# Four-layer hybrid decoder on one core: where the sums of squares stand among the memory products, and who adds the squares

## The reference

```
def rms_norm(x, g):
    xf = x.astype(F32)
    y = xf * lax.rsqrt(jnp.mean(xf * xf, axis=-1, keepdims=True) + EPS)
    return (y * g.astype(F32)).astype(x.dtype)

def memory_kv(mem, g, w_k, w_v):
    m = rms_norm(mem, g)
    shp = mem.shape[:2] + (X_HEADS, X_HEAD_DIM)
    return (m @ w_k).reshape(shp), (m @ w_v).reshape(shp)
...
        x = x + rms_norm(y, g[1])
        h = rms_norm(x, g[2])
        y = memory_cross_attn(h, mem_k[layer], mem_v[layer], P['x_w_q'][layer], P['x_w_o'][layer])
        x = x + rms_norm(y, g[3])
```

## Time and profile before

| | us |
|---|---|
| median of 3 runs | 2017.05 |
| lowest and highest run | 2014.43, 2022.57 |
| span of the profiled execution | 2015.7 |
| TensorE busy | 1951.5 (97%) |
| VectorE busy | 1244.4 (62%) |
| ScalarE busy | 930.6 (46%) |
| GpSimd busy | 1008.8 (50%) |

### The profile page before, as it was taken

How to read it: one execution, slowest core, us unless ns; L and a number is a source line. 1 busy time by engine, 2 the same in 40 slices (tenths; PEclk the granted TensorE clock), 3 DMA queues, 4 the chain that set the end, 5 groups by cost and what they waited for, 6 DMA issues and landing times.

```text
span 2015.7 us, 35615 instructions
## 1 busy us (share of the span) xinstructions
PE 1951.5 (97%) x13890; PEld 1763.9 (88%) x13890; DVE 1244.4 (62%) x2220; ACT 930.6 (46%) x1557; POOL 1008.8 (50%) x1249
## 2 busy tenths in 40 slices
PE   7999999999999999999999999999999999999997
PEld 5998989798888988897889999999998889989976
DVE  5988342426887787755147777777454157874552
ACT  3676522334555555342354444443243347674333
POOL 4776704026555655250356666566631337776602
PEclk8999999999999999999999999999999999999998
DMA  4444476535444544487353444444586344445870
GB/s 130 149 147 135 135 250 231 208 105 174 124 116 132 151 132 140 138 297 241 113 170 108 130 130 130 137 136 146 165 313 211 132 148 141 135 148 166 292 231 27
DMA packets 332615, 324.64 MB, mean 161 GB/s; under 512 B 19768, under 2 KB 313056, under 8 KB 332448
## 3 DMA queue, kind: packets, MB, share of 16 engines
q1 hardware_dynamic: 330944, 321.49, 49.8%
q10 hardware_dynamic: 1504, 0.87, 0.2%
HBM read 292.16 MB, written 29.61 MB: 160 GB/s over the span
## 4 chain that ended last, share of the span: by engine, by line
PE 75%; DVE 14%; ACT 5%; issue 2%; DMA 2%; POOL 1%; SPq 1%; DVEq 0%; ACTq 0%
PE ps L773 10%; PE ps L774 10%; PE ps L778 10%; PE ps L1458 5%; PE ps L1467 4%; PE ps L1261 3%; PE ps L1524 2%; PE ps L888 2%; PE ps L763 2%; PE ps L765 2%; PE ps L764 2%; ACT wh L1713 2%; DVE work L2543 2%; PE ps L1602 1%; PE ps L1541 1%
## 5 line engine op out<-in xcount | busy, mean ns | idle before, releaser
L1693 POOL TENSOR_TENSOR wl<-raw,wh 128x256 fp32r<-128x256 f32 x1216 | 1003.3, 860 | 979.1 <-ACT wh L1713 978.9
L1713 ACT ACTIVATE wh<-raw 128x1024 fp32r<-128x1024 f32 x304 | 311.8, 1053 | 202.1 <-PE ps L778 49.8
L773 PE MATMUL ps<-Hh,wh 128*128 128x320 f32 x1200 | 372.2, 324 | 2.8 <-DVE work L2563 0.9
L774 PE MATMUL ps<-Hl,wh 128*128 128x320 f32 x1200 | 360.4, 314 | 0.0
L773 PEld LDWEIGHTS ps<-Hh,wh 128*128 128x128 f32 x1200 | 230.0, 192 | 11.3 <-DVE work L2427 2.3
L774 PEld LDWEIGHTS ps<-Hl,wh 128*128 128x128 f32 x1200 | 230.4, 192 | 2.1
L2258 DVE TENSOR_SCALAR work<-ps 128x512 f32<-128x512 f32 (+8 forms) x220 | 100.3, 474 | 170.9 <-PE ps L871 39.8
L778 PE MATMUL ps<-Hh,wl 128*128 128x320 f32 x1200 | 201.1, 310 | 0.0
L778 PEld LDWEIGHTS ps<-Hh,wl 128*128 128x128 f32 x1200 | 183.2, 189 | 0.1
L773 PE MATMUL ps<-Oh,wh 128*128 128x320 f32 x512 | 152.2, 310 | 3.7 <-DVE Ol L3004 3.7
L774 PE MATMUL ps<-Ol,wh 128*128 128x320 f32 x512 | 151.1, 308 | 0.0
(11 more groups left out here) (439 smaller groups left out, 3922.0 us busy)
## 6 DMA issues: line engine op xcount, KB each, us to landing
raw<-rg_w_in SPq DMA_DIRECT2D x128, 256.0 KB, 3.5
raw<-hg_w_in SPq DMA_DIRECT2D x128, 256.0 KB, 4.8
raw<-ssd_w_in SPq DMA_DIRECT2D x96, 256.0 KB, 3.9
work<-cache_mem_k SPq DMA_DIRECT2D x40, 512.0 KB, 6.3
work<-cache_mem_v SPq DMA_DIRECT2D x40, 512.0 KB, 5.1
raw<-rg_w_out SPq DMA_DIRECT2D x64, 256.0 KB, 3.6
raw<-x_w_k SPq DMA_DIRECT2D x64, 256.0 KB, 3.6
raw<-x_w_v SPq DMA_DIRECT2D x64, 256.0 KB, 3.7
```

The source lines that it names most:

```text
L773: pe.matmul(ps[:, bank, 0:n], high(half, k), mh[:, k, 0:n], start=(k == 0), stop=False)
L774: pe.matmul(ps[:, bank, 0:n], high(half, k), ml[:, k, 0:n], start=False, stop=False)
L1693: ins = pool.tensor_tensor(out, src, wh[:, parted(n) % HALVES, r:r + 2].bitcast(F32), ALU.subtract)
L1713: act.activation(wh[:, nx.n % HALVES], raw[:, slot, :, half * P:(half + 1) * P], ACT.Copy).then_inc(hi_ready, 1)
```

## The change

Three edits, all in the attention stages.

1. At a seam, `sum_squares(5 + 4 * L, 7)` becomes `sum_added`: VectorE adds the eight tiles of X's squares (seven additions behind its `residual`), and TensorE runs one product with ones in place of eight. The numbers of `sq_added` are counted anew (4 for each layer in place of 3). The sum moves from before the wait for `at_v_ready` to two steps of k behind it.
2. At a seam, `values(4, 0)` is cut in two: four steps of k stand before the first sum, four after it. The later `values(4, 0)` is cut at two steps around the second sum.
3. In attention 1 the first sum moves from behind `memory(0)` into the middle of `memory(1)`.

The sums write banks 6 and 7, the value products 4 and 5, the memory products 0 to 3, so a group of accumulations can stand open around a sum. ScalarE's, GpSimd's and SyncE's programs stay as they are.

```
--- before.py
+++ after.py
@@ -1441,7 +1441,7 @@
 
 
             def attention(L):
-                def memory(n):
+                def memory(n, ks=range(KD)):
                     block = units.n // 2
                     pe.wait_ge(landed[block % SLOTS], 64 * (block // SLOTS + 1))
                     if L != 1 and n < 4:
@@ -1452,21 +1452,22 @@
                         pe.wait_ge(*past("rg_so_ready", 8 * (1 if L == 0 else 2)))
                     if n >= 4:
                         pe.wait_ge(*past("at_kvt_ready", KD * L + n - 3))
-                    for k in range(KD):
+                    for k in ks:
                         if n == 0:
                             pe.wait_ge(*past("mem_normal", 2 * KD * L + k + 1))
                         mm = pe.matmul(ps[:, n % 4, 0:NMEM], raw[:, block % SLOTS, k, n % 2 * P:(n % 2 + 1) * P], memh[:, k, :],
                                        start=(k == 0), stop=(k == KD - 1))
-                    done(mm)
-
-                def values(bank, a):
+                    if KD - 1 in ks:
+                        done(mm)
+
+                def values(bank, a, ks=range(KD)):
 
                     block = units.n // 2
                     pe.wait_ge(landed[block % SLOTS], 64 * (block // SLOTS + 1))
-                    for k in range(KD):
+                    for k in ks:
                         mm = pe.matmul(ps[:, bank, 256 * a:256 * a + 256], memh[:, k, a * P:(a + 1) * P], raw[:, block % SLOTS, k, :],
                                        start=(k == 0), stop=(k == KD - 1))
-                    if a:
+                    if a and KD - 1 in ks:
                         done(mm, 2)
 
                 def turn_memory(h):
@@ -1480,11 +1481,16 @@
                             mm = pe.transpose(ps[:, 4 + h % 2, 256 * a + P * c:256 * a + P * (c + 1)], at_kt[:, t, a * P:(a + 1) * P], ident[:])
                     mm.then_inc(S("at_turned_full"), 1)
                 for n in range(KD):
-                    memory(n)
-                    if n == 0:
-                        sum_added(2 + 4 * L, 6, 3 * L + 1)
+                    if L == 1 and n == 1:
+                        memory(1, range(4))
+                        sum_added(2 + 4 * L, 6, 4 * L + 1)
+                        memory(1, range(4, KD))
+                    else:
+                        memory(n)
+                    if L != 1 and n == 0:
+                        sum_added(2 + 4 * L, 6, 4 * L + 1)
                     if n == 4:
-                        sum_added(3 + 4 * L, 7, 3 * L + 2)
+                        sum_added(3 + 4 * L, 7, 4 * L + 2)
                     if n % 2 == 1 and n >= 3:
                         turn_memory((n - 3) // 2)
                 if L == 0:
@@ -1612,16 +1618,18 @@
                         pe.wait_ge(*past("at_y_ready", KD * L + t - 3))
                     project(t % 4, t % 2, Oh, Ol)
                 if L == DEPTH - 1:
-                    sum_added(4 + 4 * L, 6, 3 * L + 3, (KD - 1,))
+                    sum_added(4 + 4 * L, 6, 4 * L + 3, (KD - 1,))
                     return
-                values(4, 0)
-                sum_added(4 + 4 * L, 6, 3 * L + 3, (KD - 1,))
+                values(4, 0, range(4))
+                sum_added(4 + 4 * L, 6, 4 * L + 3, (KD - 1,))
+                values(4, 0, range(4, KD))
                 values(4, 1)
                 values(5, 0)
                 values(5, 1)
-                sum_squares(5 + 4 * L, 7)
                 pe.wait_ge(*past("at_v_ready", XH * (L + 1) + 2))
-                values(4, 0)
+                values(4, 0, range(2))
+                sum_added(5 + 4 * L, 7, 4 * L + 4)
+                values(4, 0, range(2, KD))
                 values(4, 1)
 
             rg(0)
@@ -3004,6 +3012,8 @@
                     tt(sample_o(Ol), ps[:, 6 + hb, 0:256].rearrange("p (c h q) -> p c h q", c=2, h=XH), sample_o(Oh).bitcast(F32), SUB).then_inc(S("at_o_ready"), 1)
                 add_squares(4 + 4 * L, KD - 1)
                 residual(4 + 4 * L, gain(L, 3))
+                if L < DEPTH - 1:
+                    add_squares(5 + 4 * L)
 
                 wait("at_k_out0", (L + 1) * 32)
                 wait("at_k_out1", (L + 1) * 32)
```

## The result

| | before | after |
|---|---|---|
| median of 5 runs, us | 2017.05 | 1999.74 |
| lowest and highest, us | 2014.43, 2022.57 | 1996.85, 2007.11 |
| span of the profiled execution, us | 2015.7 | 1999.1 |
| TensorE busy, us | 1951.5 | 1935.4 |
| VectorE busy, us | 1244.4 | 1254.4 |

The ratio is 0.9925, 95% interval 0.9906 to 0.9943: 0.75% faster, 11.5 to 19 us. The forecast was faster by 10.49 us (0.52%). Its chances were nearly even, 0.47 for a gain beyond 0.5% and 0.51 for one within; the whole interval lies beyond.

A forecast was written before the change was run, and what follows sets the result against it. Seams were taken as bounded by the second sum's end plus 7.60 us, with TensorE busy 97%. Three seams at 2.91 us plus 1.76 us in attention 1 made 10.49 us: 2006.6 us forecast, range 2001.5 to 2013.5.

The forecast's parts named there:

- The bound of a seam: At each seam, the mixer starts 7.60 us after the second sum ends; 2.91 of 3.77 us removed arrive.
- The first half step: At a seam, the first sum moves 1.72 us earlier, to 430.78, its input ready 0.16 us before; no TensorE cost.
- The adds: At a seam, VectorE's seven additions run from 440.04 to 444.10 us, 0.7 us before TensorE sums, at no cost.
- C: At the seams, adds come late on slower VectorE, 6.6 us; a seam gives 1.0 us, total 2012.2 us; chance 0.06.
- Attention 1: At its start, the moved first sum fills TensorE's wait for VectorE's adds; gain 1.76 us, second sum fitting by 0.2.
- Idle time: Before the mixer, TensorE's wait grows to about 1.4 us at the first seam; weight-part waits total 4.4 us.
- B: The clock falls once at each of the three seams; 5.4 us gained, 2011.7 us; chance 0.08.
- D: The clock falls at a seam and stays low 10.4 us; 4.8 us slower, 2021.8 us; chance 0.04.
- the clock term: Clock loss at the seams' longer gaps, taken as none; the range keeps 1.7 us a seam.
- I find nothing with a fixed date: Behind the seams, waits and weight loads hang on the chain and move by the same 2.91 us, so the gain survives.
- 3 us to each side: Whole kernel: spread taken around the forecast case, for run spread and short clock falls.
- E: Behind the seams, their gain is handed back by a load or early sum; only 1.76 us stays, 2015.3; chance 0.06.

The follow-up runs named there:

- The early weight parts: Changed kernel with ScalarE making the high parts of the mixer's first two weight units before the second sum's root: ratio 0.9934, a seam of 22.62 us.
- the run with GpSimd held back: Changed kernel with those weight parts before the root and GpSimd waiting for VectorE's products with the root: ratio 0.9953, a seam of 22.15 us.

## Why the prediction was right, and where it was short

- **The bound of a seam** (end of the second sum plus 7.60 us) was right: 7.60 us after the change, 7.60 with eight products, and filling work behind the sum cost nothing. The gain was put at 2.91 us a seam and measured 2.91.
- **The first half step**: the first sum started without a wait at 430.56, forecast 430.78 less the 0.22 us by which the stage came earlier. The 0.16 us of slack that the rows of attention 3 gave were enough.
- **The adds**: forecast 4.06 us from 440.04, measured 4.06 from 439.82. Nothing was queued behind them that waited, and C, the late adds, did not happen: GpSimd's empty stretch decided that. The early weight parts made C's condition true for a part of the adds, and then they took 5.08 us; C's ratio of 1.63 would have made 6.6. The Trainium skill ("SBUF — State Buffer", section "Who interferes with whom") says that a VectorE instruction with two SBUF inputs contends with a GpSimd instruction that reads SBUF. These rows agree: 4.06 us alone, 5.08 beside GpSimd.
- **Attention 1**: forecast 1.76 us, measured 1.72. It fitted before the second sum too.
- **Idle time**: TensorE's waits for the weight parts, forecast 4.4 us in total, are in the list of waits after as shown below. TensorE's busy time was forecast at about 1940 us and came to 1935.4; three falls of the clock fewer, at about 1.4 us each, make 4.2 of the difference.

```profile
PE ps L787 <- ACT wh L1721: 4.4, 3, 1.6
```

- **Behind the seams**: the wait of 2.20 us at 470.91 moved with the chain and shrank:

```profile
467.20 1.01 PE L994 MATMUL ps<-smallc,work 128*128 128x32 f32 x6 [1.82 <-ACT work L1871]
```

  In the fourth mixer TensorE's waits for VectorE grew, from 1.0 to 2.1 us: one of the prediction's own signs of being wrong. Two rows of the waits after, in its first 147 us, that the same stretch before does not have:

```profile
PE ps L773 <- DVE work L2435: 0.7, 2, 0.4
PE ps L888 <- DVE work L2266: 0.4, 1, 0.4
```

- **Rivals B and D of the prediction** (the clock falls at the seams): no fall stood at a seam in the profile after, nor in any other of the fourteen; apart from the start and the end of the program all stood in the second and third mixers. The longer gap had dense products on both sides, as in the row at 857 us.
- **The terms that failed are the clock term, taken as none, and "I find nothing with a fixed date"**, which put the rest of the kernel at nothing. The measured 15 us (by the ratio) are 10.4 from the change's own stretches. Behind the seams the runs showed three things in place of nothing: 2.7 us of clock by the mean over all runs (three falls fewer in the profile after, eight for eleven), 2.2 us less idle time in the third mixer, and 1.36 us handed back in the fourth. So the sum was right for what it added up, and short of the total by 4.6 us, by effects that it had not priced; these three make 3.5 of them, and where the rest lies stays open.
- **The width**: "3 us to each side". The median of after, 1999.74, lies 1.8 us below the low end, 2001.5; by the ratio on the median of before it would be 2001.9, just inside. I had seen the mean clock of 0.96 in the third mixer and named falls that come and go, but gave all of them together the weight of less than two. That the total lies at the edge of the range is luck: the low end was made from the full removed work and a fall or two, and the full removed work did not come.
- **Not foreseen**: 1.36 us were handed back in the fourth mixer (next section but one). E had named a seam's gain handed back, by a load or by the projection's squares, but the whole of it; it was neither, and a part.

## What to carry to other kernels

At a hand-over between engines, look for the last result that the chain waits for and price the gain by how much earlier that result comes, not by the work taken away: here 3.77 us of products left a seam and 2.91 arrived, and 1.3 us of work could be put back for nothing. Splitting a block of filling work around a short dependent product is a cheap way to bring the product to the date at which its input is ready, and worth doing up to that date and no further. Before a seam is shortened again, ask what the stage behind it hangs on: three kernels shortened the first seam by another 1.3 to 1.7 us, and the second mixer gave all of it back; behind the third seam, shortened by 1.5 to 2.0 us, the fourth mixer took 213.7 to 214.6 us in place of 212.2 to 212.6.

## What the runs showed of the hardware

- GpSimd and VectorE cost each other time when both read two operands from SBUF: seven adds took 4.06 us alone and 5.08 beside GpSimd for part of the time, eight products with the root 3.79, 4.64 and in attention 1 6.16 us, eight low parts 5.49 and 7.11 us. In the last case, in the run with GpSimd held back, the engines took turns, one instruction each in 0.95 us: VectorE's took 1.02 us in place of 0.49, GpSimd's 0.98 in place of 0.73.
- The same effect probably made a stage longer when its weights came earlier. In the fourth mixer one iteration on VectorE was 18.03 us in the profile before, where ScalarE had waited 2.27 us for the landing of a weight block and GpSimd started late on it, and 20.17 us in the profile after, where ScalarE waited 1.14 us and GpSimd worked beside two VectorE instructions, as it does in other iterations of both. With the two short rows ahead of them (0.28 and 0.25 us before, 0.76 and 0.81 after) they make 2.14 us:

```profile
1716.57 0.81 DVE L2431 TENSOR_TENSOR work<-work 128x640 f32<-128x640 f32 x1
1717.30 0.81 DVE L2433 SCALAR_TENSOR_TENSOR work<-work 128x640 f32<-128x640 f32 x1
```

```profile
1699.44 1.37 DVE L2439 TENSOR_TENSOR work<-work 128x640 f32<-128x640 f32 x1
1700.73 1.36 DVE L2441 SCALAR_TENSOR_TENSOR work<-work 128x640 f32<-128x640 f32 x1
```

  The first two rows are before, the last two after. GpSimd's four instructions at the same place, before and after:

```profile
1716.94 4.47 POOL L1693 TENSOR_TENSOR wl<-raw,wh 128x256 fp32r<-128x256 f32 x4 [1.14 <-ACT wh L1713]
```

```profile
1697.77 3.63 POOL L1701 TENSOR_TENSOR wl<-raw,wh 128x256 fp32r<-128x256 f32 x4 [0.15 <-ACT wh L1721]
```

  Before they start behind VectorE's first row and take the longer time themselves; after they are there first. That this is the cause of the 1.36 us is read from the rows; no run tested it alone. That something is handed back is steady: the fourth mixer took 210.2 to 211.2 us in the three profiles with eight products at the seams, 212.2 to 212.6 in the eight with the adds and the weight parts at their old place.
- TensorE's clock differs between executions of one program here: in 23 runs of the kernel before on one chip, the mean clock went from 0.982, with a span of 2020.4 us, to 0.988, with 2007.8; in three profiles of the changed kernel it fell eight, eight and ten times behind the start. A difference of 0.3% between two such kernels needs the mean clock beside it.
